# Row sums of the modulation vector that scales the experts' output, moved from the recurrence to the last block of the experts' second products

## What is computed

```python
def first_block(x, c, ...):
    mod = (jax.nn.silu(c) @ w_ada[l] + b_ada[l])[:, None, :]
    sh1, sc1, gt1, sh2, sc2, gt2 = jnp.split(mod, 6, axis=-1)
    xn = rms_norm(h, norm1_g[l]) * (1.0 + sc1) + sh1
    ...                                   # projections, attention, RWKV recurrence
    h = h + gt1 * (mixed @ w_out[l])
    xn2 = rms_norm(h, norm2_g[l]) * (1.0 + sc2) + sh2
    h = h + gt2 * peer_ffn(xn2, ...)      # experts: gelu(x u^T) * gate, times v
    return h
```

## Time and profile before

| what | us |
|---|---|
| median of three runs | 1719.4 |
| the profiled execution: span from first to last instruction | 1714.4 |
| the median run less that span (start and end) | 5.0 |
| PE busy | 1638.3 (96%) |
| DVE busy | 1134.8 (66%) |
| ACT busy | 816.7 (48%) |
| POOL busy | 123.8 (7%) |
| PE's share of the chain of waits | 85% |
| DVE's share of the chain of waits | 8% |

### The profile page before, as it was taken

One profiled execution on the slowest core, in us unless ns is written; L12 is line 12 of the kernel. 1 busy time (PEld: TensorE's weight loads), 2 busy tenths in 40 slices (PEclk: granted clock), 3 DMA queues, 4 the chain that ended last, 5 costly groups with the idle time before them and its releaser, 6 DMA issues.

```text
span 1714.4 us, 27220 instructions
## 1 busy us (share of the span) xinstructions
PE 1638.3 (96%) x11462; PEld 1492.9 (87%) x11462; DVE 1134.8 (66%) x1969; ACT 816.7 (48%) x1183; POOL 123.8 (7%) x54
## 2 busy tenths in 40 slices
PE   6999988979999999999999999999999998999998
PEld 4889876979999999998899888888898787999996
DVE  5784865654699889996544676555675464556675
ACT  4745434334454444444444544444434755455663
POOL 0001232000648000000000000000000000000000
PEclk8999988989999999999999999999999998999999
DMA  9534323334455555455655686555754443445331
GB/s 396 210 126 167 111 99 128 129 138 151 170 172 197 175 182 173 161 184 180 215 207 175 214 290 221 190 191 194 272 194 154 145 152 134 166 158 171 127 130 63
DMA packets 48460, 300.56 MB, mean 175 GB/s; under 512 B 5585, under 2 KB 6097, under 8 KB 15826
## 3 DMA queue, kind: packets, MB, share of 16 engines
q1 hardware_dynamic: 43442, 290.28, 48.1%
q10 hardware_dynamic: 4896, 8.54, 1.3%
HBM read 288.18 MB, written 9.44 MB: 174 GB/s over the span
## 4 chain that ended last, share of the span: by engine, by line
PE 85%; DVE 8%; ACT 4%; DMA 2%; issue 1%; SPq 0%; DVEq 0%; ACTq 0%
PE ps L597 84%; DVE WL L1949 2%; DVE ar L1922 1%; ACT ar L1349 1%; DVE ar L1933 1%; DMA ar<-in_ada 1%; DVE ar L2249 1%; ACT WH L1357 1%; DMA vec<-in_vec 0%; DMA ar<-in_in_rkv 0%; PE ps L778 0%; ACT L1349 0%; DVE ar L1941 0%; DVE ar L2078 0%; DVE RL L1965 0%
## 5 line engine op out<-in xcount | busy, mean ns | idle before, releaser
L1949 DVE TENSOR_TENSOR WL<-ar,WH 128x1024 fp32r<-128x1024 f32 (+1 forms) x428 | 503.2, 1204 | 334.9 <-ACT WH L1357 334.1
L597 PE MATMUL ps<-RH,WH 128*128 128x256 f32 x2136 | 629.5, 295 | 21.0 <-DVE WL L1949 6.7
L597 PE MATMUL ps<-RL,WH 128*128 128x256 f32 x2136 | 611.7, 286 | 0.0
L597 PE MATMUL ps<-RH,WL 128*128 128x256 f32 x2136 | 611.2, 286 | 0.0
L1357 ACT ACTIVATE WH<-ar 128x1024 fp32r<-128x1024 f32 (+1 forms) x478 | 481.7, 1042 | 263.6 <-PE ps L597 248.2
L597 PEld LDWEIGHTS ps<-RH,WH 128*128 128x128 f32 x2136 | 417.1, 195 | 27.7 <-DVE WL L1949 8.1
L597 PEld LDWEIGHTS ps<-RL,WH 128*128 128x128 f32 x2136 | 417.7, 196 | 0.9 <-issue 0.2
L597 PEld LDWEIGHTS ps<-RH,WL 128*128 128x128 f32 x2136 | 417.1, 195 | 0.0
L597 PE MATMUL ps<-WH,RH 128*128 128x512 f32 (+1 forms) x832 | 323.8, 389 | 7.4 <-DVE RL L2443 4.3
L597 PE MATMUL ps<-WL,RH 128*128 128x512 f32 (+1 forms) x832 | 320.4, 385 | 0.0
L597 PE MATMUL ps<-WH,RL 128*128 128x512 f32 (+1 forms) x832 | 320.4, 385 | 0.0
(11 more groups left out here) (155 smaller groups left out, 941.6 us busy)
## 6 DMA issues: line engine op xcount, KB each, us to landing
ar<-in_u SPq DMA_DIRECT2D x64, 1024.0 KB, 4.9
ar<-in_v SPq DMA_DIRECT2D x64, 1024.0 KB, 4.9
ar<-in_adr SPq DMA_DIRECT2D x16, 1024.0 KB, 5.5
ar<-in_ada SPq DMA_DIRECT2D x8, 1024.0 KB, 12.5
ar<-in_in_g SPq DMA_DIRECT2D x8, 1024.0 KB, 4.9
ar<-in_wq SPq DMA_DIRECT2D x8, 1024.0 KB, 4.9
far_gates<-ar ACTq DMA_DIRECT2D x32, 256.0 KB, 2.0
ar<-far_gates SPq DMA_DIRECT2D x16, 512.0 KB, 3.8
```

Of the source, the lines that this page charges most:

```text
L597: ins = q.matmul(o, l, r, start=start and i == 0, stop=stop and i == len(pairs) - 1, skip_group_check=skip)
L1949: q.tensor_tensor(l[:, x:z, :], src[:, x:z, :], h[:, x:z, :].bitcast(F32), ALU.subtract).then_inc(*v.up(("lo", n, i)))
```

## The change

The last four `adr` chunks (`LATE`) leave the recurrence. Their transfers and their four pairs of row sums stand in the last block of second products, behind chunks 1, 3, 5 and 7. Since `cwide` is overwritten by then, silu(c) is made again: SP loads it once more, ACT makes the sigmoid, DVE the product.

```diff
-DOTS = ((0, 0, 0, 2, 0, 0, 0, 2, 0, 2, 0, 2), (0, 2, 0, 0) * 2 + (0, 2) * 2, (0, 2, 0, 0) * 2 + (0, 2) + (0,) * 6)
+DOTS = ((0, 0, 0, 2, 0, 0, 0, 2, 0, 2, 0, 2), (0, 2, 0, 0) * 3, (0,) * 16)
+LATE = (12, 13, 14, 15)
...
+def late_after(name, b, j):
+
+    return name == "v" and b == 3 and j in (1, 3, 5, 7)
...
@@ chunk_order @@
-        seq += [(n, 16 * b + j) for j in range(16)]
+        for j in range(16):
+            seq += [(n, 16 * b + j)] + ([("adr", LATE[j // 2])] if late_after(n, b, j) else [])
@@ chunk_slots @@
-    mixed = range(CHUNKS.index(("in_v", 0)), CHUNKS.index(("adr", 15)) + 1)
+    mixed = range(CHUNKS.index(("in_v", 0)), CHUNKS.index(("adr", LATE[0] - 1)) + 1)
...
@@ peer (memory) @@
         self.gate_in = [ar[:, at + 1024 * k:at + 1024 * k + 1024] for k in range(4)]
+        self.cwide_late, self.c_sigmoid_late = self.gate_in[0:2]
...
@@ scalar_program, down @@
+            if b_ == 3 and r == 0:
+                a.wait_ge(m.c_load, 32)
+                AC(m.c_sigmoid_late, m.cwide_late, ACT.Sigmoid, "late c sigmoid")
+            yield
+            yield
+            yield
+            yield
+            if late_after("v", b_, r):
+                feed.take()
...
@@ vector_program, front @@
-        TT(mod[:, 16:48], mod[:, 16:48], vc("b_ada", 16, 32), ALU.add)
+        TT(mod[:, 16:40], mod[:, 16:40], vc("b_ada", 16, 24), ALU.add)
...
@@ vector_program, dot_chunks @@
+        for j in range(LATE[0]):
+            yield from dots_of(j, m.cwide, "c wide silu")
+
+    def dots_of(j, silu, need):
+
+        feed.take()
+        c = CHUNKS.index(("adr", j))
+        w = m.chunk(c)
+        v.wait_ge(*m.loaded(c))
+        for f in range(2):
+            x, i = w[:, 1024 * f:1024 * f + 1024], 16 + 2 * j + f
+            v.wait_ge(*on(need))
+            q.scalar_tensor_tensor(x, x, 1.0, silu, ALU.mult, ALU.mult,
+                                   accum_out=mod[:, i:i + 1]).then_inc(*v.up(("adr", j)))
+            yield
...
@@ vector_program, down @@
+            if b_ == 3 and r == 1:
+                v.wait_ge(*on("late c sigmoid"))
+                TT(m.cwide_late, m.cwide_late, m.c_sigmoid_late, ALU.mult, "late c silu")
+            yield
+            yield
+            yield
+            yield
+            if late_after("v", b_, r):
+                finish(dots_of(LATE[r // 2], m.cwide_late, "late c silu"))
+                if r == 7:
+                    TT(mod[:, 40:48], mod[:, 40:48], vc("b_ada", 40, 8), ALU.add)
...
@@ sync_program @@
+        if (name, j) == ("v", 40):
+            s.wait_ge(*on(("gated", 1)))
+            q.dma_start(m.cwide_late, m.D["cwide"]).then_inc(m.c_load, 16)
```

More of the change, by code:

```diff
@@ L78, in front_order @@
 def front_order():
-    dots = iter([x for j in range(16) for x in (("adr", j), None)])
+    dots = iter([x for j in range(LATE[0]) for x in (("adr", j), None)])
     seq = []
@@ L170, in dma_order @@
 def dma_order():
-    lo, hi = CHUNKS.index(("in_v", 0)), CHUNKS.index(("adr", 15)) + 1
+    lo, hi = CHUNKS.index(("in_v", 0)), CHUNKS.index(("adr", LATE[0] - 1)) + 1
     def free(c):
@@ L1101, in dot_chunks @@
     def dot_chunks():
-        for _ in range(16):
+        for _ in range(LATE[0]):
             feed.take()
@@ L2874, in sync_program @@
     s.wait_ge(m.lora_loads, 80)
-    s.wait_ge(m.c_load, 16)
+    s.wait_ge(m.c_load, 32)
     s.wait_ge(m.table_loads, 48)
```

## The result

| | us |
|---|---|
| before, median of 20 runs | 1719.5 (1717.5 to 1725.7) |
| changed, median of 20 runs | 1725.2 (1719.7 to 1740.8) |
| ratio, 95% interval | 1.0041 (1.0022 to 1.0060) |
| changed, the profiled execution: span | 1721.5 (its time 1723.3) |
| before, the profiled execution: span | 1714.4 |

The change costs 4 to 10 us, 7 by the ratio; the forecast was 11.5. In every run whose span is known, the time is 1.8 to 1.9 us above the span, not 5.0: so the profiled execution of the kernel before took about 1716.3 us, some 3 us less than the median, and the 5.0 us of its table are not start and end alone. The page first: its chain by engine, and the row of the matmuls that begin a chunk of second products (what they were released by stands behind the last bar).

A forecast was written before the change was run, and what follows sets the result against it. PE was taken as the bound (busy 96%, 85% of the chain of waits). The last block costs 18.9 + 0.7 + 0.4 = 20.0 us, the recurrence returns 8.5: +11.5, so 1719.4 becomes 1731, own range 1724 to 1737.

The forecast's parts named there:

- Rival C: Last block: SP's queue does not hold PE, each pair costs only its 0.35 us slip; 1712 us, chance 0.09.
- Rival E: Recurrence: moved in_g transfers make the split at 212.58 late beyond its 2.3 us slack; 1739 us, chance 0.05.
- Rival D: Last block: stalls 2 us deeper each from clock or late third transfer, recurrence gives only 3; 1743 us, chance 0.06.
- The first stall: Last block: PE starts chunk 4 at T2+16.2, 5.55 us lost; T2 is when PE is done with chunk 1.
- Term (e): Last block: matmuls run at a lower clock behind an idle PE; 0.7 us lost, bounds 0 to 4.
- The slips: Last block: each of four pairs on DVE ahead of the low hidden values delays PE 0.35 us, 1.4 together.
- (a): Recurrence: first pair off the chain and POOL's passes moved with the in_g chunk 5 split; 2.9 us less, 1.1 to 3.5.
- (d): Recurrence: PE's granted clock, 0.57 over 270-286 and 297-305, rises; 2.5 us less, bounds -2 and 10.
- less than 5 or more than 12: Sign of being wrong: the recurrence gives back less than 5 or more than 12 us, where 8.5 was forecast.
- rival B: Recurrence gives back as much as the block loses, its ceiling of 17 us; 1722 us, chance 0.10.
- (b): Recurrence: second pair off the chain, limited by scores PE ends at 266.04; 1.4 us less, bounds 0 and 2.29.
- (c): Recurrence: in_g chunk 7's split no longer precedes the heads' high part and the squares; 1.7 us less, at most 3.4.

The follow-up runs named there:

- own_hold: Changed kernel with late adr chunks in memory of their own, each transfer still waiting for the previous pair: 1723.5 us; without that wait 1706.6 us.
- queue_order: Changed kernel, but SP issues adr13, adr14 and adr15 behind the two v chunks that follow them instead of ahead: 1709.3 us, ratio 0.9931.
- block_only: Kernel before with all 16 chunks in its recurrence, plus chunks 12 to 15 a second time through the ring in the last block: 1739.7 us, ratio 1.0106.
- no_late: Changed kernel with the four last adr chunks left out altogether, neither transfers nor row sums: 1706.8 us, 14.2 below the kernel before.
- thin_pairs: Kernel before with row sums of chunks 12 to 15 over 8 of 1024 columns, transfers and split order kept: 1719.8 us, ratio 1.0003.
- pairs_back: Changed kernel without late transfers and row sums, with eight dummy row sums on DVE at the old recurrence places: 1716.2 us, ratio 0.9971.
- fill: Changed kernel with late chunks in own memory, unheld, single row sums, plus three constant matmuls at PE's recurrence state waits: 1709.7 us, ratio 0.9932.

## Why the prediction was right, point by point

**The mechanism of the loss** was right at each step, and own_hold (one wait added) and queue_order (three transfers moved) show that it is the cause. Rival C (the queue does not hold PE) needed v52 to be issued before the pair of adr12 is done; it was issued 0.39 us after (1138.57 against 1138.18). Rival E (the moved `in_g` transfers eat the gain) did not occur: the split that was at 212.58 is at 216.51, later by 3.9 us, which is the late start and nothing more. Rival D foresaw that the third transfer of a burst, or the clock, makes a stall deeper; v56 did land 8.59 us after its issue, where v52 took 7.63 and v54 6.81, against 7.0 from the earlier trace rows.

**Its size.** The first stall: PE restarts at T2+16.8, forecast T2+16.2, the difference being v52's landing. The next, by the distances of restarts less 10.88: 4.96 (5.2 forecast) and 6.74 (5.2). Before chunk 10 it is 2.5 in the second profile (PE restarts at 1180.73 and 1194.13), 2.6 in block_only and 2.75 in queue_order (2.75 forecast). By the block stretch the block costs 20.65 us in the first profile of the changed kernel, 19.8 in the second and 20.1 in block_only, where 18.9 for the stalls and 0.7 for the clock were forecast; by the medians block_only costs 18.8, with 20.0 forecast. Term (e), the clock behind a stall, was named rightly: it is 0.50 behind the first and third stall, and 2.7 us of the second one (4.96 less the 2.28 of its wait) pass in slow matmuls of the round. The slips were mis-sized, 0.22 instead of 0.35 us, which matters little.

Why v56 is late, the DMA view of 1130:1200 shows in part (busy tenths and GB/s of 40 slices of 1.75 us):

```profile
DMA  0000079999100047999200056999400004799998
GB/s 0 14 0 5 0 108 389 407 426 412 56 0 0 0 75 323 407 435 435 122 0 0 0 70 267 440 398 431 187 14 0 0 0 66 272 417 431 435 248 351
```

The three bursts move the same sum in about the same six slices. So the third burst is no slower as a whole by more than a part of a slice; its second transfer is done later within it. What orders them inside a burst stays open. The Trainium skill, DMA: Bandwidth & Descriptors, Where 436 GB/s comes from, says that for transfers from HBM the memory side binds at about 358 GB/s for a core, and that 435 is the ceiling of the SBUF side. The trace differs on the first: these are transfers from HBM, and full slices show 389 to 440 GB/s, with one core at work. It agrees with the second to within 1%, by which the highest slice is above it. The same section also gives 425 GB/s for one transfer of 16 MB.

**The recurrence.** This is the step that was mis-sized: "(a) to (d): 8.5 us less". It measured 14.2 by the medians (no_late, 12.0 to 17.7) and 17.2 in the profile. The prediction had named "less than 5 or more than 12" as a sign of being wrong, and by that sign this step was wrong. The ceiling of 17 was reached, as rival B had it. Up to the second pair the terms were sound: counted from the first tanh, the 80 matmuls behind it come 35.58 us later before (270.49) and 30.69 in the changed kernel (269.58), 4.9 less, where (a) and (b) make 4.3. The other 12.3 come after it, for which (c) and (d) had 4.2.

POOL's part of (a) went as forecast: its passes run from 240.51 to 245.20, which less the 3.97 of late start is 236.5 to 241.2, and they meet the product on DVE, the row below, 0.85 us instead of 0.42 for the same product.

```profile
244.63 0.85 DVE L1937 TENSOR_TENSOR ar<-ar,small 128x256 f32<-128x256 f32 x1
```

The Trainium skill, GPSIMD Engine Reference, Specifications, says that VectorE instructions with two SBUF inputs contend with GpSimd; this product has two, and the trace agrees, 0.43 us for one meeting.

What failed is the treatment of (d), the clock, as one term beside the others with a value of 2.5. In the tanh stretch PE's busy time for the same matmuls fell by 9.5 us; its waits fell by 7.8, where (a) to (c) have 6.0. Two stretches of 16 and 8 us at 0.57 went to 1.00. I had the ceiling of 10 worked out and took a quarter of it because "whether shorter gaps keep the clock up no row shows". thin_pairs and pairs_back show that neither edit brings it alone (0 and 4.8 us at the median, 3.9 and 4.8 at the higher clock), and both together do (14.2); the clock over the stretch is 0.74, 0.87 and 0.95 in the profiles, 0.82 before. A price for each edit and a sum over them could not find that. What in the two edits keeps the clock up stays open.

**The sum.** By the medians 18.8 less 14.2 is +4.6, by the profile 20.65 less 17.2 is +3.4, and the two sets of runs of the changed kernel gave +7.1 and +5.3 by their ratios, which hold its runs at the low clock too; its fifteen other runs are +4.3. These agree within the intervals. The forecast of +11.5 was above all of them, by the recurrence's 5.7 or more. The time, 1725.2, lies nearer to rival B's 1722, which had a chance of 0.10, than to the forecast's 1731, and only 1.2 us inside the prediction's own range of 1724 to 1737. The sign was not luck: the block's loss was sized well and is larger than even the ceiling of the gain. That the range held in spite of a gain beyond "more than 12" is partly luck. The upper end of the runs, 1740.8, goes with the lowest mean clock (0.965), and the one profile of that recurrence at a low clock is 14.5 us longer; that it is not deeper stalls is argued from this, since no such run of the changed kernel was profiled.

## What to carry to other kernels

A transfer with a wait of its own, put into an in-order queue, costs what stands behind it: before placing it, ask which instruction its wait hangs on and when the next transfer in the queue was due. Here pairs of 2.4 us on an engine with half its time free stopped TensorE three times for 5 to 7 us and once for 2.5, and moving three transfers back by two places cured most of it. Read a chain of stalls by the distance between restarts, since slow matmuls behind a wait hide part of it. Where the granted clock is low beside the edit, do not price it as a small term: forecast with both clocks, and keep the range that wide. And look whether a filler meets the waits that it is meant for before reading its time as an answer: fill's did not.

## What the runs showed of the hardware that was not expected

- The same 816 matmuls in the same order took 69.3 or 83.8 us (PE busy 64.5 or 81.6), by whether the granted clock was low from about 251 to 258 us or from 243 to 290. Over the whole execution the mean clock was 0.965 to 0.970 in the changed kernel's runs above 1730 us, and 0.973 to 0.981 in those below 1727.
- Of two edits beside the recurrence one gained 0 us at the median (3.9 in its runs at the higher clock) and the other 4.8, and both together 14.2.
- Constant matmuls put in front of one kind of wait added 6.1 us of work, took away 1.2 us of idle time, and left the mean clock of the stretch at 0.95; its low spell moved from 250 to 258 us to about 261 to 268.
- Beside a pass of POOL a row sum of 128x1024 on DVE took 3.29 us instead of 1.21 (pairs_back against before), and a product of 128x256 0.85 instead of 0.42. Another row sum beside POOL, at 244.61 in the kernel before, kept its 1.22 us, and there POOL's two passes took 5.46 instead of 4.74.
- When three transfers of 1 MB were issued in a row, the second landed 7.63, 6.81 and 8.59 us after its issue, in three bursts of one execution.
